# Two expert layers of a hybrid decoder: lists read at the end of the routing, first gathers ahead of the fills

## What is computed

```python
def hier_moe(x, norm_w, w_group, w_expert, w_gate, w_up, w_down):
    h = rmsnorm(x, norm_w)                 # 2048 x 1024
    g_sel = argmax(h @ w_group)            # one of 4 groups
    top_p, top_e = top_k(softmax(expert logits of that group), 2)
    eid = g_sel * 8 + top_e                # two of 32 experts for each token
    # tokens sorted by expert, padded to blocks of 128 rows
    def expert_block(xblk, e):
        return (silu(xblk @ w_gate[e]) * (xblk @ w_up[e])) @ w_down[e]   # 1024 -> 256 -> 1024
    out = scatter-add of block outputs times the token's weight
```

## Time and profile before

| what | us |
|---|---|
| three runs, median | 2975.74 |
| three runs, lowest and highest | 2974.16 and 2978.79 |
| the profiled execution, its own time | 2978.49 |
| span of its trace | 2976.8 |
| PE matmul busy | 2613.8 (88%) |
| DVE busy | 1798.3 (60%) |
| ACT busy | 1665.1 (56%) |
| POOL busy | 592.4 (20%) |
| layer one: end of the routing's last DVE step, first expert product | 1017.5 and 1042.5 |
| layer two: the same | 2345.9 and 2370.0 |

### The profile page before, as it was taken

One profiled execution on the slowest core, in us unless ns is written; L12 is line 12 of the kernel. 1 busy time (PEld: TensorE's weight loads), 2 busy tenths in 40 slices (PEclk: granted clock), 3 DMA queues, 4 the chain that ended last, 5 costly groups with the idle time before them and its releaser, 6 DMA issues. The chain is left out here.

```text
span 2976.8 us, 41675 instructions
## 1 busy us (share of the span) xinstructions
PE 2613.8 (88%) x12246; PEld 2098.0 (70%) x12246; DVE 1798.3 (60%) x3153; ACT 1665.1 (56%) x2276; POOL 592.4 (20%) x795
## 2 busy tenths in 40 slices
PE   6999999999799589999994999998799589999840
PEld 4878878788688467777773888886688467777730
DVE  4555655554365566556654888876456576555636
ACT  5556656545344366556653777776344376555632
POOL 0000000000011254554440000000011245555420
PEclk9999999999899799999996999999899799999975
DMA  3322322341344489789775555451445599878867
GB/s 114 100 93 81 111 92 78 93 148 57 123 156 147 168 282 325 257 302 322 269 259 212 175 178 193 143 187 57 144 155 163 171 360 340 286 249 279 300 245 291
DMA packets 388257, 573.60 MB, mean 193 GB/s; under 512 B 33408, under 2 KB 304000, under 8 KB 384000
## 3 DMA queue, kind: packets, MB, share of 16 engines
q1 hardware_dynamic: 353104, 457.23, 46.5%
q0 software_dynamic: 32688, 105.99, 9.6%
q10 hardware_dynamic: 2304, 8.39, 0.7%
HBM read 449.32 MB, written 122.22 MB: 192 GB/s over the span
## 5 line engine op out<-in xcount | busy, mean ns | idle before, releaser
L1445 DVE TENSOR_TENSOR experts_gu_lo<-carry_raw,experts_gu_hi 128x1024 fp32r<-128x1024 f32 x256 | 296.7, 1222 | 63.8 <-ACT experts_gu_hi L1404 62.5
L118 PE MATMUL experts_ps<-experts_gu_hi,experts_hT_hi 128*128 128x512 f32 x760 | 316.8, 417 | 2.9 <-issue 2.9
L1327 POOL DMA_INDIRECT experts_rows<-h_rows,experts_source_now x194 | 262.2, 1352 | 266.2 <-PE experts_ps L1497 135.0
L119 PE MATMUL experts_ps<-experts_gu_lo,experts_hT_hi 128*128 128x512 f32 x760 | 300.8, 396 | 0.0
L120 PE MATMUL experts_ps<-experts_gu_hi,experts_hT_lo 128*128 128x512 f32 x760 | 300.4, 395 | 0.0
L1404 ACT ACTIVATE experts_gu_hi<-carry_raw 128x1024 fp32r<-128x1024 f32 x256 | 250.2, 1056 | 51.0 <-DMA carry_raw<-in_moe_w_up 41.4
L1456 DVE TENSOR_TENSOR experts_hT_lo<-experts_ps,experts_hT_hi 128x512 fp32r<-128x512 f32 x194 | 133.5, 688 | 236.8 <-ACT experts_hT_hi L1383 235.7
L963 POOL MEMSET route_empty<- 128x512 int32 x2 | 1.1, 564 | 1287.7 <-POOLq L160 1287.7
L118 PE MATMUL route_ps<-route_w_hi,route_src_hi 128*128 128x512 f32 x512 | 209.0, 408 | 41.8 <-DVE route_src_lo L1029 41.8
L1396 ACT ACTIVATE experts_y<-experts_ps,experts_by_block 128x1024 f32<-128x1024 f32 x99 | 110.7, 1118 | 211.6 <-DMA y_rows<-experts_y,experts_target_now 211.3
L119 PE MATMUL route_ps<-route_w_lo,route_src_hi 128*128 128x512 f32 x512 | 203.7, 398 | 0.0
(11 more groups left out here) (322 smaller groups left out, 6755.8 us busy)
## 6 DMA issues: line engine op xcount, KB each, us to landing
carry_raw<-in_moe_w_gate SPq DMA_DIRECT2D x64, 1024.0 KB, 11.0
carry_raw<-in_moe_w_up SPq DMA_DIRECT2D x64, 1024.0 KB, 12.8
ahead_wd_raw<-in_moe_w_down SPq DMA_DIRECT2D x64, 1024.0 KB, 6.1
gla_w_raw<-in_gla_w_in SPq DMA_DIRECT2D x32, 1024.0 KB, 7.3
ahead_wd_raw<-in_lru_w_in SPq DMA_DIRECT2D x32, 1024.0 KB, 8.3
gla_w_raw<-in_gla_w_in SPq DMA_DIRECT2D x32, 512.0 KB, 5.1
route_src<-oT_rows SPq DMA_DIRECT2D x32, 512.0 KB, 4.2
x_rows<-route_x_new SPq DMA_DIRECT2D x32, 512.0 KB, 2.9
```

The lines of the kernel that those rows point to most:

```text
L118: nc.tensor.matmul(out, w_hi, x_hi, start=first, stop=False)
L119: nc.tensor.matmul(out, w_hi, x_lo, start=False, stop=False)
L1327: pool.indirect_dma_start(rows[:, b], None, h_halves[b], bass.IndirectOffsetOnAxis(source_now[b][:].bitcast(U32), 0))\
L1445: nc.vector.tensor_tensor(gu_lo[:, slot(e), of_part(c)], gu_raw[:, slot(e), of_part(c)], gu_hi[:, slot(e), of_part(c)].bitcast(F32), ALU.s ...
```

## The change

Six edits, the same for both layers since the code is shared:

1. The read of the lists and the making of `sources` move from `experts` into the end of `project_and_route`: SP waits for the scatters (POOL did before), reads the table into `ahead.lists`, DVE makes all row numbers in one instruction.
2. In `experts` POOL names and gathers both halves of the first block right behind its two smallest fills. The other fills follow the gathers, and so do the two large fills of `wd_hi` and `wd_lo`, which move from DVE to POOL.
3. ACT splits the first gate/up weights at once, ahead of the table load for the silu function, and waits for the fills behind that. DVE likewise.
4. PE no longer runs the 12 products with zeros. DVE fills the two PSUM banks with zeros instead, and counts as the product on the semaphore `y_ps_done`.
5. The wait for the `wd` fills moves to where they are first read or overwritten: PE in expert 0 ahead of its down product, ACT ahead of the split of expert 1's down weights.
6. `lists` and `sources` now live on into the recurrence, so the recurrence's `h` and `square` use their space, and `LruEarly` is made behind the routing.

```diff
@@ project_and_route, SP
                 sp.wait_ge(h_stored[j], nth_store(NT - 1))
+            for j in range(2):
+                sp.wait_ge(scattered[j], NT * DMA)
+            sp.dma_start(ahead.lists[:], lists_out.rearrange("(p n) o -> p n o", p=P)).then_inc(ahead.lists_in, DMA)
@@ project_and_route, POOL
             tiles(pool, body)
-            for j in range(2):
-                pool.wait_ge(scattered[j], NT * DMA)
@@ project_and_route, DVE
             step(nc.vector.tensor_copy(k.blocks[:], packed[:]))
+            dve.wait_ge(ahead.lists_in, DMA)
+            nc.vector.tensor_scalar(ahead.sources[:], ahead.lists[:, :, 0], 1, T - 1,
+                                    ALU.logical_shift_right, ALU.bitwise_and)\
+                .then_inc(ahead.sources_set, 1)
@@ experts, SP
             m.prime(sp)
-            sp.dma_start(lists[:], lists_dram.rearrange("(p n) o -> p n o", p=P)).then_inc(lists_in, DMA)
@@ experts, POOL
-            pool.memset(by_block[:, 0:LAG, 1], 0)
-            pool.memset(y[:], 0.0)
-            pool.memset(aT_hi[:].bitcast(F32), 0.0)
-            pool.memset(aT_lo[:].bitcast(F32), 0.0)
-            pool.memset(act_[:], 0.0).then_inc(zeroed, 1)
-            pool.wait_ge(zeroed, 1)
+            pool.memset(by_block[:, 0:LAG, 1], 0).then_inc(first_set, 1)
...
             for b in range(2):
                 name_rows(b, 0, 0)
                 gather(b, 0)
+            pool.memset(act_[:], 0.0)
+            pool.memset(aT_hi[:].bitcast(F32), 0.0)
+            pool.memset(aT_lo[:].bitcast(F32), 0.0)
+            pool.memset(y[:], 0.0).then_inc(zeroed, 1)
+            pool.memset(wd_hi[:, 1].bitcast(F32), 0.0)
+            pool.memset(wd_lo[:, 1].bitcast(F32), 0.0).then_inc(wd_zeroed, 1)
+            pool.wait_ge(first_set, 1)
+            pool.wait_ge(zeroed, 1)
             keep_list(0, 0)
             name_targets(-2)
             store_y(-2)
-            pool.wait_ge(sources_set, 2)
@@ experts, ACT
-            act.wait_ge(zeroed, 1)
-            act.wait_ge(wd_zeroed, 1)
-
+            split_gu(0)
             nc.scalar.activation(silu[:, 0:1], k.eps[:], ACT.Silu).then_inc(table_in, 1)
             act.wait_ge(table_in, 1)
-            split_gu(0)
+            act.wait_ge(zeroed, 1)
...
                     split_gu(e + 1)
+                if e == 1:
+                    act.wait_ge(wd_zeroed, 1)
                 split_wd(e, first)
@@ experts, DVE
-            nc.vector.memset(wd_hi[:, 1].bitcast(F32), 0.0)
-            nc.vector.memset(wd_lo[:, 1].bitcast(F32), 0.0).then_inc(wd_zeroed, 1)
-            dve.wait_ge(lists_in, nth_dma(0))
-            for columns in (slice(0, 1), slice(1, E * SLOTS)):
-                nc.vector.tensor_scalar(sources[:, columns], lists[:, columns, 0], 1, T - 1,
-                                        ALU.logical_shift_right, ALU.bitwise_and).then_inc(sources_set, 1)
-            dve.wait_ge(zeroed, 1)
+            dve.wait_ge(y_ps_done, nth(-1))
+            nc.vector.memset(ps[:, Y:Y + 2], 0.0).then_inc(y_ps_done, 1)
             split_gu(0)
             for b in range(2):
                 take_rows(0, b)
+            dve.wait_ge(zeroed, 1)
@@ experts, PE
-            pe.wait_ge(zeroed, 1)
-            pe.wait_ge(wd_zeroed, 1)
             for b in range(2):
                 transpose_rows(0, b)
-            down(0, 1)
+            pe.wait_ge(zeroed, 1)
             transpose_act(0)
...
                 pe.wait_ge(aT_lo_done, nth(g))
+                if e == 0:
+                    pe.wait_ge(wd_zeroed, 1)
                 pe.wait_ge(wd_lo_done, nth(made))
```

21 lines of the change are left out of this document (12 added, 9 removed).

## The result

The changed kernel takes 2993.24 us, the median of 8 executions (2984.84 to 2996.48), against 2980.01 for the kernel before (8 executions, 2974.16 to 2986.45): a ratio of 1.0040, 95% interval 1.0029 to 1.0050. It is **slower by 0.4%**, outside the predicted range. The profiled execution of the change took 2996.04 us, with a span of 2994.3 us against 2976.8. Single executions of one kernel spread over some 12 us, so medians carry the verdicts and traces carry the mechanisms.

What follows compares the result with a forecast made beforehand. The prediction took the start as a race between PE's queue and POOL's gathers, with POOL last. Layer one's +3.7 and layer two's +0.7 gave +4.4 us on the median 2975.74, so 2980.1, range 2969 to 2988.

Steps and rivals of the forecast that it cites:

- they are hidden: Layer one's start: seven first gate/up products at the slow clock, 1.4 us, covered by PE's wait for POOL, adding nothing.
- layer two's +0.7: Layer two: bytes limit and leave up to 3.0 us earlier, partly taking back PE's delay; -3.0 to +3.7, taken +0.7.
- The border, +1.2: Between routing and experts: SP waits for the scatters and reads the lists, so the border opens 1.2 us later, at 1024.9.
- The first gathers, -3.0: POOL at the experts' start: first naming 3.3 us earlier, second gather 2.4 to 3.3 us earlier, taken as 3.0.
- The first product at 1039.5: PE's first gate/up product in layer one moves 3.0 us earlier, from 1042.53 to 1039.5, at clock 0.50.
- POOL's fills, +1.8: POOL behind the first gathers: fills of 5.3 us together make the next block's naming and gather 1.8 us later.
- The collision, +3.7: Layer one: the next block's second gather falls inside the 3 MB weight load; late rows cost +0.4 to +3.7, taken +3.7.
- POOL as the bound of both starts: Slower rival: gathers collide in both layers, slow clock unhidden, PE limits layer two, nothing taken back; +10, 2986; chance 0.17.
- No collision: Rival: the gather gets its share beside the weights, rows come at 1053.1, +0.4 a layer, 2976.5; chance 0.13.
- The head start is kept: Faster rival: the fills don't hold the next block's gathers, so -3.0 a layer stays, -6.0, 2969.5; chance 0.22.
- not as described: Rival: the list read waits for more than the scatters, border opens at 1028 or later, +5 a layer, 2986; chance 0.03.

Runs made afterwards that it cites:

- the kernel before with POOL's fills: Kernel before plus seven POOL fills of 512 elements (unread buffer, 4.04 us together) between first gathers and first list column: 2994.18 us, 1.0045.

## Why the prediction was wrong

The mechanism was right in layer one. Two steps failed: "they are hidden", which put the slow clock at nothing, and, above all, layer two's +0.7, which let the bytes leave earlier and take the delay back. Step by step, with the predicted value first:

- **The border, +1.2.** Held. The list read left at 1020.15, 2.19 us behind the last scatter (2.2 assumed), the border opened at 1025.72, +1.2 net of the routing's drift, and POOL's drain was hidden, though not as described: it began at 1016.5 and took 5.23 us instead of 2.75.
- **The first gathers, -3.0.** Failed by half: the first naming came 3.4 us earlier net (3.3 forecast), but the second gather only 1.4. The step counted the first gather at its length from before, 1.03 us; it took 2.27, beside the split of the weights that DVE had begun at 1027.81, and it was issued 0.6 us later behind its naming than before. I had priced a drawn-out *naming* and not a drawn-out *gather*. The Trainium skill, "SBUF — State Buffer", section "Who interferes with whom", lets a DVE instruction with two SBUF inputs hold off a GpSimd instruction that reads SBUF, and a gather reads its row numbers there. The traces agree in the main. In the kernel before, none of the 90 gathers that lie clear of DVE's weight splits lasted over 1.03 us, and of the 104 beside one 53 lasted over 1.5. In the change the store at 1047.76, which reads its targets there, lasts 2.17 us with DVE's two-input split of `wd` (2.29 us) running from 1046.77, and the first fill, at 1032.14, begins 0.3 us before DVE's split ends and lasts 0.33 like the next two. But a split doesn't always draw a gather out: the one at 1045.50 lies inside DVE's split of 1042.22 to 1046.85 and took 1.09 us. What decides there stays open.
- **The first product at 1039.5.** It was 1040.62, 2.7 earlier net (3.0 forecast), cold as forecast. That the number came out is partly luck: the second transposes moved by 1.6 net and not by 3.0 (1034.65 against 1035.50), and PE's queue then read the block table in 5.1 us where it had taken 6.1.
- **POOL's fills, +1.8.** The size of the fills held, 5.15 us for the six (5.3 forecast). The naming was +2.2 net and the first rows +1.6 (+1.8 forecast), and that is two errors that nearly cancel: the list column was kept 3.5 us later net (2.3 forecast), since the gathers ahead of the fills had lost their time, and from there to the naming it took 7.1 us, where I had 7.9.
- **The collision, +3.7.** The rows of the second half came 5.7 us behind the end of their gather (6.7 behind its start) and 8.6 behind the weights' issue (7.2 and 9.2 in the row that I had taken). The weights left 1.8 us earlier net, not 3.0, so the rows were at +5.7 net, against +5.2 for that end. Less the wait of 1.50 that is no longer paid, that is +4.2.
- **"They are hidden", the slow clock.** This step failed in layer one. I had seven products at the slow clock, covered by PE's wait. All twelve of the first half ran at it, and these were covered. But the waits of 2.91 and 3.70 us kept the clock low through most of the second half and the whole down product: twelve products, one every 0.43 us instead of 0.23, 2.4 us, behind the last wait, where nothing covers them. 4.2 + 2.4 = 6.6, and the trace has 7.3 less 0.77 at block 2. So the sum for layer one was +3.7 and measured about +6.6 in this execution. Of the two terms the slow clock is an effect of the waits for rows: the kernel before with POOL's fills is warm at its first product and loses as much.
- **Layer two, +0.7.** This was the largest error. POOL's last scatter in layer two, before and in the change:

```profile
2345.57 0.97 POOL L975 DMA_INDIRECT expert_lists<-route_entry,route_place_int  x1 [0.30 <-issue]
```

```profile
2355.87 0.97 POOL L978 DMA_INDIRECT expert_lists<-route_entry,route_place_int  x1 [0.30 <-issue]
```

  It is 10.3 us later, and block 72 is 17.5 later, so layer two itself costs +7.2 where the term had +0.7. At its first product (2377.77 against 2370.0) the layer still has a head start of 2.5 us net, as in layer one. I had argued that bytes limit there and that the bytes would leave 3 us *earlier*. For SP's second load that held, 2.0 us earlier net (2386.15 against 2377.90). The third left 5.8 us *later* net (2404.32 against 2388.23), 18.2 us after the second instead of 10.3:

```profile
2377.90 0.37 SPq L1290 DMA_DIRECT2D ahead_wd_raw<-in_moe_w_down  x1
...
2388.23 0.37 SPq L1290 DMA_DIRECT2D ahead_wd_raw<-in_moe_w_down  x1
```

```profile
2386.15 0.37 SPq L1293 DMA_DIRECT2D ahead_wd_raw<-in_moe_w_down  x1
...
2404.32 0.37 SPq L1293 DMA_DIRECT2D ahead_wd_raw<-in_moe_w_down  x1
```

  The chain is in ACT's order. Behind ACT's output instruction stands its step on the second half's rows, behind that the split of the next expert, DVE's split behind that, and SP's third load behind DVE's. In the change two late transfers hold it within a microsecond of each other: the output waits for the store until 2393.85, and PE transposes the late rows at 2394.74, which ACT takes at 2395.78:

```profile
2393.85 1.11 ACT L1401 ACTIVATE experts_y<-experts_ps,experts_by_block 128x1024 f32<-128x1024 f32 x1 [10.42 <-DMA y_rows<-experts_y,experts_target_now]
...
2396.28 3.89 ACT L1409 ACTIVATE experts_gu_hi<-carry_raw 128x1024 fp32r<-128x1024 f32 x4
```

  The rows are enough by themselves. With one large fill on DVE the store is in time and the gather isn't, and the third load still leaves 19.4 us behind the second (2390.71 and 2410.09). ACT's timeline there:

```profile
2391.96 1.12 ACT L1400 ACTIVATE experts_y<-experts_ps,experts_by_block 128x1024 f32<-128x1024 f32 x1 [3.52 <-DMA y_rows<-experts_y,experts_target_now]
...
2400.95 0.60 ACT L1387 ACTIVATE experts_hT_hi<-experts_ps 128x512 fp32r<-128x512 f32 x1 [7.11 <-PE experts_ps L1499]
```

  Ahead of the third load of the change the DMA engines run short of work. The window in front of it, and the one of before that lies as far behind the last scatter:

```profile
2398.00:2404.00 6.00, 6.00 (x30) 4.80 (x30) 5.99 (x5) 5.86 (x7) 2.90 (x3) 0.97 0.65 227
```

```profile
2388.00:2394.00 6.00, 6.00 (x24) 4.88 (x24) 2.11 (x5) 3.05 (x5) 2.90 (x6) 0.75 1.05 397
```

  The share is 0.65 against 1.05. In layer one the same gap (30.1 us between SP's second and third load, 21.7 before) cost nothing more, and there the engines had time left (0.21). In layer two the lost bytes aren't made good: the difference is +17.5 at block 72 and +17.7 at block 96. The kernel before with POOL's fills alone shows the same 18.2 us between the two loads (2385.94 and 2404.11), and with the fills on DVE there are 10.3 again (2377.98 and 2388.23).
- **The rivals.** The nearest was the slower one, POOL as the bound of both starts (+10); the measurement is +13.2. Its first two conditions came in. Its third, PE and not DMA as the limit in layer two, was not needed: the DMA share of 2408 to 2500 is 0.97 with PE busy 83.78 of 92. *No collision* fell with the 6.7 us of the gather. *The head start is kept* fell in the change, where it is gone by block 0, and with it *not as described*: the border opened at 1025.72 and not at 1028.

The large part is measured twice: the large fills on POOL cost +12.8 us in the change (against itself with them on DVE), and fills on POOL in the kernel before cost +14.9 (2994.18 against 2979.33). The small parts, -3.1 for edit 1 and +3.4 for edit 4, are each as wide as their interval of some 3 us to either side. All three add up to +13.1, where +13.2 was measured, but with such intervals an agreement to 0.1 us is luck. What is left for the gathers ahead of the fills, edit 2's other half, is near nothing: the version with the fills on DVE has it and lies 0.0 from before. It wasn't run alone.

Still open is why one fill on POOL costs no less than two, and why the distance to the kernel before drifts by up to 6 us in mid layer in kernels that differ only at the start.

## What to carry to other kernels

Before work is put on an engine because it is "idle", ask what DMAs that engine issues next, and where they fall against the bulk loads: 3.7 us of fills moved a gather from 2.5 us ahead of a 3 MB load to 1.9 us behind it and a store to 1.3 us ahead of it, and these then took 6.7 and 9.1 us where they had taken under 4. Follow the late transfer in every in-order queue up to the next load that it releases; where bytes limit, a load that leaves late costs about its whole delay. And test a large edit part by part: here one part gave 0.1%, one took 0.1%, and two moved lines took 0.4%. And before two traces are compared, take off the distance that they have where the changed code begins: here it came to 10.3 us in layer two.

## What the runs showed of the hardware

- An indirect DMA on POOL took 2.27 us beside DVE's weight split at 1027.81, where the median of the 194 gathers in the kernel before is 1.00. Of these the 90 clear of DVE's weight splits took 1.03 at most, and 53 of the 104 beside one took over 1.5.
- A gather of 128 rows issued 1.9 us behind a 3 MB load landed 6.7 us later; 2.6 us ahead of the load it took at most 3.6 (1045.57 to 1049.16, fills on DVE). With one large fill on POOL, 0.9 us behind the load, it took 8.0 (1051.33 to 1059.32). A store issued 1.3 us ahead took 9.1 us (1047.76 to 1056.84), and one issued 2.5 us ahead took at most 3.8 (1048.01 to 1051.76).
- The clock did not stay up for having been raised. With the fast clock at the first product (0.47 us a product) and then waits of 5.54 and 2.69 us for rows, the granted clock of 1052 to 1066 was 0.80; in the kernel before, with waits of 1.04, 1.18 and 1.50 us, it was 1.00.
